# A decoder layer's last normalisation: the scaling of a token tile moved from VectorE to ScalarE and GpSimd

## What is computed

```
x = h + sum over j of gate_j * e_j
out = x * rsqrt(mean(x * x) + 1e-5) * norm_final_g
```

## Time and profile before

| what | us |
|---|---|
| median of 3 runs | 3139.24 |
| lowest and highest run | 3136.91, 3139.30 |
| the profiled execution | 3134.6 |
| its span, from the first to the last instruction | 3133.0 |
| DVE busy in the span | 1096.0 (35%) |
| ACT busy in the span | 658.9 (21%) |
| POOL busy in the span | 513.7 (16%) |
| PE busy in the span | 2770.1 (88%) |

### The profile page before, as it was taken

The page is one execution under the profiler, slowest core; times in us unless marked ns, Lnnn a source line. Parts: engine busy times, 40 slices in busy tenths (PEclk is TensorE's granted clock), DMA queues, the critical chain, the costliest instruction groups (busy, mean ns, idle before and its releaser), DMA issues. The chain is left out here.

```text
span 3133.0 us, 52814 instructions
## 1 busy us (share of the span) xinstructions
PE 2770.1 (88%) x19900; PEld 2601.8 (83%) x19901; DVE 1096.0 (35%) x2470; ACT 658.9 (21%) x1243; POOL 513.7 (16%) x745
## 2 busy tenths in 40 slices
PE   7898897788987889794999999999999999999980
PEld 6885686378887878794999999999999999999980
DVE  2118422455554413353232213223232232222228
ACT  3118511323322213220111111111111111111111
POOL 0000000442430000034212121121211212112104
PEclk9998999798988999896999999999999999999995
DMA  7110111000003020217888778888888888887867
GB/s 240 31 34 1 34 51 30 8 20 18 16 13 115 8 80 1 63 62 245 290 288 288 261 257 292 289 297 292 282 297 294 289 290 295 293 289 268 280 238 275
DMA packets 340495, 549.52 MB, mean 175 GB/s; under 512 B 41120, under 2 KB 120864, under 8 KB 340384
## 3 DMA queue, kind: packets, MB, share of 16 engines
q1 hardware_dynamic: 321056, 505.56, 47.3%
q0 software_dynamic: 19360, 42.87, 4.6%
HBM read 507.06 MB, written 41.31 MB: 175 GB/s over the span
## 5 line engine op out<-in xcount | busy, mean ns | idle before, releaser
L2409 PE MATMUL experts_up<-experts_xs,g_pieces 128*128 128x144 f32 (+1 forms) x8192 | 1035.3, 289 | 75.4 <-DVE experts_xs L2338 38.9
L2409 PEld LDWEIGHTS experts_up<-experts_xs,g_pieces 128*128 128x128 f32 x8192 | 1028.6, 197 | 82.5 <-issue 82.5
L2432 PE MATMUL experts_down<-experts_hs,g_across 128*128 128x144 f32 (+1 forms) x3072 | 389.2, 288 | 0.0
L2432 PEld LDWEIGHTS experts_down<-experts_hs,g_across 128*128 128x128 f32 x3072 | 386.1, 190 | 0.0
L2291 POOL DMA_INDIRECT experts_x<-h_rows,experts_index x198 | 191.7, 968 | 1133.3 <-DVE experts_xs L2338 1078.4
L2368 DVE TENSOR_SCALAR experts_glu<-experts_up,experts_bias 128x176 f32<-128x176 f32 x256 | 102.3, 400 | 710.5 <-PE experts_up L2409 710.5
L2318 ACT ACTIVATE experts_sig<-experts_glu 128x352 f32<-128x352 f32 x128 | 63.6, 497 | 961.7 <-DVE experts_lin L2370 961.7
L2325 ACT ACTIVATE experts_yT<-experts_down,experts_bias 128x176 f32<-128x176 f32 x256 | 104.5, 408 | 380.8 <-PE experts_down L2432 305.6
L2359 DVE COPY experts_bias<-g_bias 128x24 f32 x32 | 5.8, 180 | 391.7 <-ACT experts_yT L2325 391.6
L2421 PE MATMUL experts_down<-experts_hs,g_across 128*128 128x144 f32 (+1 forms) x1024 | 133.2, 288 | 0.0
L2421 PEld LDWEIGHTS experts_down<-experts_hs,g_across 128*128 128x128 f32 x1024 | 130.1, 190 | 0.0
(11 more groups left out here) (415 smaller groups left out, 4136.2 us busy)
## 6 DMA issues: line engine op xcount, KB each, us to landing
g_pieces<-in_w_dram SPq DMA_DIRECT2D x132, 2048.0 KB, 8.1
g_across<-in_w_dram SPq DMA_DIRECT2D x64, 2048.0 KB, 9.5
y_rows<-experts_y SPq DMA_DIRECT2D x132, 192.0 KB, 3.8
g_across<-in_w_ckv_dram SPq DMA_DIRECT2D x8, 1024.0 KB, 10.2
rkv_raw<-in_w_in_dram SPq DMA_DIRECT2D x13, 512.0 KB, 3.9
diff_qk_raw<-in_w_in_dram SPq DMA_DIRECT2D x9, 512.0 KB, 3.9
cross_q_raw<-in_w_cq_dram SPq DMA_DIRECT2D x9, 512.0 KB, 4.2
m_u<-in_x_dram SPq DMA_DIRECT2D x8, 512.0 KB, 9.9
```

Source lines behind the costliest of these rows:

```text
L2409: ins = pe.matmul(up[:, u % 4, l * N:l * N + w], raw[c][:, k, at:at + 255:2], xs[:, k, 0:w], start=(k == 0), stop=(k == 7), skip_group_che ...
L2432: ins = pe.matmul(down[:, n % 4, 0:w], raw[4 + n // 4][:, k, (n % 4) * P:(n % 4 + 1) * P], hs[:, k, 0:w], start=(k == 0), stop=(k == 7), s ...
```

## The change

The scaling instruction of VectorE goes. In its place ScalarE multiplies the tile by the inverse root (`even`, an activation of the kind Copy with a scale per partition, in place), and GpSimd multiplies the result by the gains vector (`gain`, a multiply in place). VectorE keeps mean and reciprocal. SyncE's store of a tile now waits for GpSimd's multiply. The wait for the gains moves from VectorE to GpSimd.

On ScalarE `even(t)` stands behind the root of tile `t`, ahead of the squares of tile `t + 1`. On GpSimd the first four multiplies stand ahead of the first gather of tiles 4 to 7 (the multiply of tile `t - 4` ahead of the gathers of tile `t`), and the last four behind all gathers.

```diff
-        scaled = S.steps("scaled", ["mean", "inverse", "scale"], back=1)
+        scaled = S.steps("scaled", ["mean", "inverse"], back=1)
+        evened, gained = S.steps("evened", ["tile"]), S.steps("gained", ["tile"])
...
             def _(pool):
+                pool.sem_inc(gained.sem, gained.start)
+
+                def gain(t):
+                    if t == 0:
+                        pool.wait_ge(gain_in, 16)
+                    pool.wait_ge(evened.sem, evened.value("tile", t))
+                    tile = x[:, t * D:(t + 1) * D]
+                    pool.tensor_tensor(tile, tile, gains[:], ALU.mult).then_inc(*gained.step("tile"))
                 for n in range(N):
+                    if n % TOPK == 0 and n >= 2 * SLOTS:
+                        gain(n // TOPK - 4)
                     if n >= SLOTS:
                         pool.wait_ge(added.sem, added.value(f"add{n % TOPK}", n // TOPK - SLOTS // TOPK))
                     pool.indirect_dma_start(rows[:, n % SLOTS, :], None, y_rows[0:WINDOW + TOPK * T_ALL, :],
                                             bass.IndirectOffsetOnAxis(ap=R.row[:, n:n + 1], axis=0)).then_inc(gathered[n % SLOTS], 16)
+                for t in range(TT - 4, TT):
+                    gain(t)
...
             def _(dve):
-                dve.wait_ge(gain_in, 16)
...
                     dve.reciprocal(stat[:, 3, t:t + 1], stat[:, 2, t:t + 1]).then_inc(*scaled.step("inverse"))
-                    dve.wait_ge(scaled.sem, scaled.so_far(t))
-                    dve.scalar_tensor_tensor(tile, tile, stat[:, 3, t:t + 1], gains[:], ALU.mult, ALU.mult).then_inc(*scaled.step("scale"))
...
             def _(act):
+                act.sem_inc(evened.sem, evened.start)
+
+                def even(t):
+                    act.wait_ge(scaled.sem, scaled.value("inverse", t))
+                    tile = x[:, t * D:(t + 1) * D]
+                    act.activation(tile, tile, ACT.Copy, scale=stat[:, 3, t:t + 1]).then_inc(*evened.step("tile"))
...
                     act.activation(stat[:, 2, t:t + 1], stat[:, 1, t:t + 1], ACT.Sqrt).then_inc(*squared.step("root"))
+                    even(t)
...
             def _(sp):
-                    sp.wait_ge(scaled.sem, scaled.value("scale", t))
+                    sp.wait_ge(gained.sem, gained.value("tile", t))
```

More of the change, by code:

```diff
@@ L2489, in scale @@
                 def scale(t):
-                    tile = x[:, t * D:(t + 1) * D]
                     scaled.round()
```

## The result

The changed kernel took 3151.49 us in the median of 12 runs (3140.97 to 3162.5), the kernel before 3139.89 in as many beside it (3134.6 to 3151.36): 11.6 us more, a ratio of 1.0040 with a 95% interval of 1.0028 to 1.0053. Two further comparisons of the same two kernels gave 1.0019 (1.0006 to 1.0032) and 1.0017 (1.0005 to 1.0029), 6.5 us each between the medians. So it is slower, as forecast, and the size of the first measurement lies just outside the range (3151.49 against 3151.3).

A forecast was written before the change was run, and what follows sets the result against it. VectorE's closed loop of adds, mean, reciprocal and scaling was taken to bound the last block. -7.2 (scaling) + 12.4 (held adds) + 3.35 (tail) = +8.5 us on the median gave 3147.7 us, range 3142.5 to 3151.3.

The forecast's parts named there:

- parts 1 and 3: Last block: scaling leaves VectorE, 7.2 us off; six GpSimd multiplies each hold VectorE's adds 2.06 us, 12.4 us on.
- rival A: Last block: GpSimd's multiplies and VectorE's two-input adds exclude each other, +8.5 us in all, 3147.7 us; chance 0.76.
- Rival B: Beside the adds: they slip past GpSimd's multiply, VectorE hardly loses, the saving stays, -3.9 us, 3135.4; chance 0.12.
- Rival C: VectorE's pause for mean and root: 0.5 us of a hold lies there, leaving 1.55; +5.5 us, 3144.7; chance 0.07.
- D: ScalarE reloads its table for copy and root: three in the tail, +3.8 us more, 3151.5; with other mishaps, chance 0.05.
- The saving: Between adds: six scalings of 1.20 us come off VectorE's path, 7.2 us.
- The hold: Adds beside GpSimd's multiply: VectorE loses 2.06 us per multiply, bounds 1.73 to 2.34, six times 12.4 us.
- part 5: After the last add: ScalarE's copies and GpSimd's last multiply end the tail 3.35 us later, bounds 3.0 to 3.9.
- The prediction's sign for the tail: End of the block: 6.4 to 6.5 us from last add to last multiply's end, where 3.6 stood.
- part 4: GpSimd's gathers behind a multiply lag 0.1 us, have some 5 us of cover, and cost nothing.
- a microsecond at either end for the spread of runs: Whole kernel: widening added to the summed bounds of 3145.4 to 3150.1 us to cover variation between runs.

## Why the prediction was right and where it failed

**The mechanism (parts 1 and 3, rival A)** was right: six adds of 2.4 us, six multiplies of 2.5, an exclusion that depends on two SBUF inputs of the one and reads of the other. Rival B (adds slip past the multiply), which had 0.12, fell on the first row of the profile after. Rival C (holds of 1.5) and D fell too: the holds are 1.90, and the block has one table load, as before.

**The saving** was a little larger: 8.72 - 7.41 = 1.31 us a tile instead of 1.20. The prediction counted the scaling's time in the chain alone. The next add now follows the reciprocal 0.08 us after its start (3119.08 and 3119.16), where the scaling followed it after 0.20.

**The hold** was a little smaller: 1.90 instead of 2.06. What the earlier trace rows gave seems to have been the right length of the exclusion, and not all of it falls on working time: the multiply, having waited for the last add of a group, begins its reading near the pause of 0.1 us between two groups of adds, which is then not lost. That is argued from the times of the chain; no run varied the pause alone. The two runs in which GpSimd waited for the scaling instead, behind which the adds follow without a pause, fit it: there the hold is the instruction's length less 0.25 to 0.27 us (1.64 of 1.89, 0.78 of 1.05). The sum of both: 6 x (1.90 - 1.31) = 3.5 us instead of 5.2.

**The tail** (part 5) came out at 3.31 against 3.35, and within it the copy at 1.15 against 1.14 and the multiply at 2.34 against 2.34. ScalarE's copy was sized right by the row that was nearest in both memory and operands. The prediction's sign for the tail, 6.4 to 6.5 us from the last add to the last multiply's end, doesn't follow from its own times: 3133.30 - 3126.32 is 6.98, and 6.94 was measured.

**The gathers** (part 4) cost nothing, as said. In the changed kernel no add waited for a row after the second group of the first tile.

**The rule of the Trainium skill** (SBUF — State Buffer, Who interferes with whom) proved good guidance in what contends: two SBUF inputs against reads of SBUF, not against writes, shown here by 2.12 us adds beside a multiply, 0.48 beside a memset and 0.49 with the sums in PSUM. Its "whole instruction" (the same page, SBUF: two separate sides) was too much: by it six holds of 2.34, measured 1.90.

**What failed** is the last step of the sum, "a microsecond at either end for the spread of runs", on a median of three. It took those three runs, 2.4 us apart, for the spread. In twelve runs the kernel before spread over 17 us (3134.6 to 3151.36) and the changed one over 22, and the median of before was 3139.89, 0.65 above the 3139.24 on which the forecast stands. Against the kernel beside it the change is 11.6 us, and the range's end allowed 12.1 (3151.3 - 3139.24): on which side of its end the value fell, by 0.2, was luck. This touches the size of the measured shift and not the mechanism. The forecast shift was 8.5 us; the block shows 6.7 to 7.6, and two comparisons 6.5. The first gave 11.6, and the value fell 0.2 us above the range's end. So the block was forecast 1 to 2 us too dear, and the measurement came out 4 us above the block. In the profiled pair the rest lies in the stretch ahead of the block, where no instruction differs; that stretch moves by up to 14 us between profiles. For the medians this is inferred, since one run of twelve was profiled. What makes it move, and whether the first comparison met it by chance alone, stays open: its interval (from 1.0028) doesn't reach the 1.0024 of the block, and the two later ones lie under 1.002. Gaps of its size between medians and blocks are not rare (-3.9 us for the multiply back on VectorE, -3.3 for the memsets), so chance would do. The repeats found no sign that the change itself reaches ahead of its block.

The shares of outcomes don't quite follow from the prediction's words either: nine tenths of A and the whole of D are 0.73, not 0.71.

## What to carry to other kernels

Work moved from VectorE to GpSimd is only off VectorE if the two don't meet at SBUF: where VectorE's instructions beside it read two SBUF tensors, each GpSimd instruction that reads SBUF costs VectorE most of its own length (here 0.42 us of 0.72, 0.78 of 1.05, 1.90 of 2.34), and a hold of 1.90 us is more than the 1.31 that the scaling had cost there. Keep one of VectorE's inputs in PSUM, or give GpSimd only work that reads nothing, and the same split pays (here 7.6 to 7.9 us of the block, 0.2 to 0.3% of the kernel). And let the pipeline's last tiles stay on the shortest path: what hides under the next tile's work has no cover in the tail.

## What was unexpected about the hardware

- An add with its sum in PSUM, read and written, costs nearly the same as in SBUF: 0.483 us against 0.478.
- A GpSimd multiply whose two inputs are one and the same tensor, with its output in another, took 1.95 us beside adds where one in place with two tensors took 2.52. Which of the two differences counts is open.
- A GpSimd instruction doesn't exclude over its whole length: 0.27 us less for a copy of 1.05, 0.3 less for a multiply of 0.72, 0.25 less for one of 1.89, 0.44 less for one of 2.34 (as seen in what the add lost).
- The same code ahead of the block ends anywhere from 3046.8 to 3060.9 us, and the longer ones mostly had a lower mean granted clock of TensorE over the whole span (0.941 at 3046.8, 0.934 at 3060.7). That is more than the change under study.
